# Two half-width GpSimd subtractions in place of one for the low parts of projection weights and keys

## What is computed

```
proj = x @ w_in                      # 5120 columns: q, k, v of two attentions, two gates
qa, ka, va -> stick_breaking(8 heads of 64)
    z = q k^T / 8;  a = exp(log_sigmoid(z) + suffix sum of log_sigmoid(-z));  y = a v
qb, kb, vb -> rope -> differential(4 heads, two maps each)
    w = softmax(z1) - lam * softmax(z2);  y = w v;  rms_norm
merged = sigmoid(ga) * (ya @ w_branch_a) + sigmoid(gb) * (yb @ w_branch_b)
x = layer_norm(ALPHA * x + merged @ w_out)
x = layer_norm(ALPHA * x + relu(x @ w_ff1)**2 @ w_ff2)
```

## Time and profile before

| | |
|---|---|
| time, median of 3 runs | 1521.79 us (1521.19 to 1521.81) |
| the profiled execution's own time | 1519.07 us |
| its span, first to last instruction | 1516.9 us |
| PE busy | 1475.1 us, 97% |
| DVE busy | 1007.9 us, 66% |
| ACT busy | 666.8 us, 44% |
| POOL busy | 328.2 us, 22%, 212 instructions |
| mean granted TensorE clock | 0.994 of full speed |

### The profile page before, as it was taken

How to read it: one execution, slowest core, us unless ns; L and a number is a source line. 1 busy time by engine, 2 the same in 40 slices (tenths; PEclk the granted TensorE clock), 3 DMA queues, 4 the chain that set the end, 5 groups by cost and what they waited for, 6 DMA issues and landing times. The chain is left out here.

```text
span 1516.9 us, 19312 instructions
## 1 busy us (share of the span) xinstructions
PE 1475.1 (97%) x7152; PEld 1226.8 (81%) x7152; DVE 1007.9 (66%) x1232; ACT 666.8 (44%) x1035; POOL 328.2 (22%) x212
## 2 busy tenths in 40 slices
PE   8999999999999998999999999999999999999997
PEld 7788888887887787888787877888888888888886
DVE  3677877779866556553346688766665467668767
ACT  3455554546556555443021344444444344433343
POOL 2535444446432223210130140000000000000004
PEclk9999999999999999998999999999999999999999
DMA  5101112111110000110452233644442677935553
GB/s 177 56 29 57 56 43 70 55 55 56 43 57 28 29 14 28 39 48 12 136 183 107 89 110 116 217 153 153 153 153 97 215 275 256 325 137 194 194 196 137
DMA packets 111503, 172.40 MB, mean 114 GB/s; under 512 B 6080, under 2 KB 71616, under 8 KB 111296
## 3 DMA queue, kind: packets, MB, share of 16 engines
q1 hardware_dynamic: 111424, 171.33, 33.2%
HBM read 127.27 MB, written 44.04 MB: 113 GB/s over the span
## 5 line engine op out<-in xcount | busy, mean ns | idle before, releaser
L756 PE MATMUL p_proj<-xt_h,w_hi 128*128 128x512 f32 x640 | 254.6, 398 | 0.2 <-DVE xt_l L1589 0.2
L760 PE MATMUL p_proj<-xt_h,w_lo 128*128 128x512 f32 x640 | 253.5, 396 | 0.0
L758 PE MATMUL p_proj<-xt_l,w_hi 128*128 128x512 f32 x640 | 252.1, 394 | 0.0
L2265 POOL TENSOR_TENSOR w_lo<-w_raw,w_hi 128x1024 fp32r<-128x1024 f32 x48 | 120.4, 2508 | 240.2 <-DVE w_hi L1596 239.7
L760 PEld LDWEIGHTS p_proj<-xt_h,w_lo 128*128 128x128 f32 x640 | 120.8, 189 | 23.6
L756 PEld LDWEIGHTS p_proj<-xt_h,w_hi 128*128 128x128 f32 x640 | 120.8, 189 | 22.4 <-DVE xt_l L1589 0.6
L758 PEld LDWEIGHTS p_proj<-xt_l,w_hi 128*128 128x128 f32 x640 | 120.9, 189 | 20.7
L2378 POOL TENSOR_TENSOR row_odd<-row_odd,gains 128x1024 f32<-128x1024 f32 x4 | 10.4, 2622 | 580.7 <-ACT row_odd L1561 580.7
L1589 DVE TENSOR_TENSOR d_al<-f_a,d_ah 128x1024 fp32r<-128x1024 f32 x56 | 68.5, 1224 | 79.5 <-ACT d_ah L1479 79.5
L1479 ACT ACTIVATE d_ah<-f_a 128x1024 fp32r<-128x1024 f32 x56 | 59.2, 1057 | 134.0 <-PE p_av L1130 54.9
L1328 ACT ACTIVATE a_t<-p_tr 128x384 fp32r<-128x384 f32 (+3 forms) x96 | 47.2, 491 | 123.4 <-PE p_tr L858 123.3
(11 more groups left out here) (287 smaller groups left out, 3537.1 us busy)
## 6 DMA issues: line engine op xcount, KB each, us to landing
f_a<-h_terms SPq DMA_DIRECT2D x56, 512.0 KB, 3.4
w_raw<-w_in SPq DMA_DIRECT2D x40, 512.0 KB, 3.9
h_terms<-c SPq DMA_DIRECT2D x40, 512.0 KB, 3.2
f_b<-w_ff SPq DMA_DIRECT2D x40, 512.0 KB, 4.9
r<-w_ff SPq DMA_DIRECT2D x32, 512.0 KB, 4.0
gate_rows<-gst SPq DMA_DIRECT2D x12, 512.0 KB, 5.0
y<-x SPq DMA_DIRECT2D x8, 512.0 KB, 7.8
wo_raw<-w_out SPq DMA_DIRECT2D x8, 512.0 KB, 8.8
```

Of the source, the lines that this page charges most:

```text
L756: pe.matmul(o, w_hi[n_slot][:, k, :], xt_h[:, k, cols], start=(k == 0), stop=False)
L758: pe.matmul(o, w_hi[n_slot][:, k, :], xt_l[:, k, cols], start=False, stop=False)
L760: mm = pe.matmul(o, w_lo[n_slot][:, k, :], xt_h[:, k, cols], start=False, stop=(k == KT - 1))
L2265: pool.tensor_tensor(w_lo[slot][:, :, :], w_raw[:, :, :], w_hi[slot][:, :, :].bitcast(F32), ALU.subtract).then_inc(wt_lo, 1)
```

## The change

POOL makes each low tile in two instructions. The 128 x 1024 subtraction of `tile_low` becomes two of 128 x 512 (the inner dimension's first four and last four blocks of 128), and the 64 x 1024 subtraction of `low_keys` two of 64 x 512 (columns 0 to 511 and 512 to 1023). The second one of each pair raises the semaphore that the single instruction raised. Nothing else differs, and the lines below it move down by two to four.

```diff
             def tile_low(n, slot):
 
                 pool.wait_ge(wt_hi, n + 1)
-                pool.tensor_tensor(w_lo[slot][:, :, :], w_raw[:, :, :], w_hi[slot][:, :, :].bitcast(F32),
-                                   ALU.subtract).then_inc(wt_lo, 1)
+                for ks in (slice(0, 4), slice(4, 8)):
+                    low = pool.tensor_tensor(w_lo[slot][:, ks, :], w_raw[:, ks, :], w_hi[slot][:, ks, :].bitcast(F32),
+                                             ALU.subtract)
+                low.then_inc(wt_lo, 1)
...
                     pool.wait_ge(st_dve, g * 4 + (m + 1))
-                    pool.tensor_tensor(k_lo[m][r, :], stage[1][r, :], k_hi[m][r, :].bitcast(F32), ALU.subtract)\
-                        .then_inc(st_pool, 1)
+                    for cols in (slice(0, NH), slice(NH, S)):
+                        low = pool.tensor_tensor(k_lo[m][r, cols], stage[1][r, cols], k_hi[m][r, cols].bitcast(F32),
+                                                 ALU.subtract)
+                    low.then_inc(st_pool, 1)
```

## The result

| | before | after |
|---|---|---|
| median of 6 runs | 1521.14 us (1518.93 to 1521.81) | 1511.40 us (1509.52 to 1513.23) |
| profiled execution | 1519.07 us | 1509.52 us |
| its span | 1516.9 us | 1507.4 us |
| mean granted clock of timed runs | 0.9932 (15 runs beside experiments 1 to 3) | 0.9965 |

What follows compares the result with a forecast made beforehand. PE, 97% busy, was taken to wait on DVE, itself held until POOL's whole instruction ended. Terms -3.3 - 0.3 - 1.3 + 0.9 - 1.7 = -5.7 us gave 1516.1 us; range 1512 to 1523.6, likeliest case 1511.8 to 1517.6.

Steps and rivals of the forecast that it cites:

- DVE gets in at the seam: Between POOL's two halves, the waiting DVE instruction goes after the first half; the forecast case, 56%.
- two rivals: DVE not let in between halves, 1523.4 us (19%); or extra instruction costs 0.36, nothing let in, 1525.8 us (7%).
- `be`, -3.3 and -0.3: PE's waits for `be`: 1.09 us sooner in each of groups 4 to 6, -3.3; group 7's wait gone, -0.3.
- `q_st`, -1.3: Group 0: DVE's cast and `q_st` alternate with POOL's halves, so PE's wait of 1.32 us goes.
- the case that the prediction named: Group 0: if POOL, not DVE's cast, goes first between the first two halves, `q_st` gains about 0.8 us.
- `a_t`, +0.9: Stick-breaking groups: DVE meets the second half, ending 0.15 us later; 0.15 charged to each of six waits.
- gains nothing: Stick-breaking groups: DVE and POOL meet at nearly every instruction, so alternating in finer pieces brings no gain.
- What a half costs, 0.15: Each POOL pair takes 0.15 us more than one whole instruction; first half 1.28 us.
- POOL busy near 345 us: Sign in the profile: POOL's busy time near 345 us, with 9.6 us from 64 splits.
- The keys' slack, 1.5 us left: Next differential group's keys end 2.7 us later than before, leaving 1.5 us before PE takes them.
- The clock, -1.7: Group 5: the fall to 1.2 GHz for 3.5 us behind the `be` wait disappears, saving 1.7 us.
- up to 3.4 us more: If timed runs held as many as three clock falls at the `be` waits, they would gain this extra.

Runs made afterwards that it cites:

- experiments 1 to 3: Changed kernel with only weight tiles halved, 1510.52 us; only key instructions halved, 1519.23; only four of 48 weight tiles halved, 1513.73; kernel before 1520.98.
- experiment 4: Only four weight tiles cut, at column 256 or at column 768 instead of 512: 1513.44 and 1514.52 us against 1521.13 for the kernel before.
- four tiles: Only the weight tile that `be` meets in each of groups 4 to 7 halved, all else whole: 1513.73 us against 1520.98 for the kernel before.
- the weights alone: Changed kernel with the keys in one instruction again, the 48 weight tiles still halved: 1510.52 us against 1520.98 for the kernel before.
- quarters: All 64 low-tile instructions in four pieces of 256 columns: 1509.58 us against 1520.98 for the kernel before, ratio 0.9927.
- Experiment 6: Kernel before plus eight discarded matmuls ahead of each of the three 2 us `be` waits: 1519.11 us against 1521.13, ratio 0.9991.
- experiment 5: Kernel before, whole POOL instructions, with DVE's cast of one weight tile per differential group issued after `be`'s L1713: 1516.02 us against 1521.13.
- both quarters: All 64 instructions in four pieces, without and with DVE's cast issued behind `be` in differential groups: 1509.58 and 1508.73 us; before, 1520.98 and 1520.66.
- Experiment 7: Sixteen discarded matmuls near 680 us, added to the kernel before with filled `be` waits and to the changed kernel: 1522.43 and 1518.86 us against 1520.66.
- experiment 2: Changed kernel with weight tiles whole again, only the 16 key instructions halved: 1519.23 us against 1520.98 for the kernel before, ratio 0.9994.

## Why the prediction was right on the waits and too small on the clock

- **DVE gets in at the seam** (56% forecast, against two rivals): right. Shown by the halves' 1.90 and 2.12 us and by the four places of the seam in experiment 4.
- **`be`, -3.3 and -0.3:** measured 6.4 to 2.9, -3.5. Group 7's wait of the earlier trace rows is gone, as said.
- **`q_st`, -1.3:** measured -0.8. It is the case that the prediction named: POOL won the first seam. Its four halves of `k_lo` ran from 40.69 to 46.75 and the cast, started at 43.97 inside a half, took 1.63 us; the wait before PE at 50.31 is 0.52.
- **`a_t`, +0.9:** the list of waits says +0.3, and in all it was a gain. The step charged a late seam to each of six waits, and four waits did rise by 0.14 or 0.15; two in group 3 fell, from 0.63 and 0.49 us to 0.36 and 0.24, by a trade of places that is shown below. From the `a_t` wait of group 2 to that of group 3 in the table above PE needs 97.38 us before and with four tiles, 96.75 with the weights alone, 96.53 with the change and 95.76 with quarters. So finer pieces do gain something in group 3, against the prediction's "gains nothing".
- **What a half costs, 0.15:** right. Two halves that meet nobody take 2.54 us against 2.39.
- **POOL busy near 345 us:** 351.7. The 9.6 us for the seams were in it; what POOL waits behind DVE was only named, and it is the rest of the rise of 23.5.
- **The keys' slack, 1.5 us left:** 1.9 left, nobody waits.
- **The waits together:** forecast -3.3 - 0.3 - 1.3 + 0.9 = -4.0. Measured -3.5 - 0.8 + 0.3 = -4.0 in the list, -5.3 in the table of matmuls, -3.6 and -4.4 at equal clock. Right in size, with some luck: `q_st` gained less and `a_t` cost less than forecast.
- **The clock, -1.7: this is the term that failed.** The mean granted clock of the timed runs rose from 0.9932 to 0.9965; 0.0033 of 1518 us is 5.0 us. This conversion is an estimate: it holds if PE works all through the falls, as the windows above show, and the 59 runs of the kernel before bear it out only roughly (4 at 0.992 average 1522.5 us, 40 at 0.993 1520.6, 12 at 0.994 1520.1, but 2 at 0.995 1521.9). The step priced the one fall of the earlier trace rows, which was gone as said. It left out the fall from 680.2 us in the same trace, which is three times as long, 10.2 us, and was 6.8 in the changed kernel's: 1.7 us that no term had. Further falls behind the `be` waits were named as a possibility, up to 3.4 us more, set in the low end and left out of the sum. Experiment 6 puts all falls behind these waits at 1.3 to 2.0 us a run, so the price of 1.7 for them was nearly right, by luck, since one execution holds one of them and another two. The other 3 us or so are at places of which the prediction said nothing.

The trade of places in group 3, in order of time; the kernel before:

```profile
347.83 0.64 POOL L2293 TENSOR_TENSOR y<-y,small 128x128 f32<-128x128 f32 x1
348.08 0.68 DVE L1680 TENSOR_TENSOR_SCAN y<-y,small 128x128 f32<-128x128 f32 x1
```

and the changed kernel:

```profile
343.62 1.51 DVE L1696 TENSOR_TENSOR y<-y 128x255 f32<-128x255 f32 x1
...
345.05 1.51 DVE L1680 TENSOR_TENSOR_SCAN y<-y,small 128x128 f32<-128x128 f32 x1
346.25 0.57 POOL L2297 TENSOR_TENSOR y<-y,small 128x128 f32<-128x128 f32 x1
...
348.03 0.41 PE L858 MATMUL p_tr<-small,y 128*128 128x128 f32 x2 [0.36 <-DVE a_t L1589]
```

Before, DVE's L1680 found POOL's `mask` (L2293) running. Now L1696, let in at the seam, is done sooner, L1680 waits behind the second half, and `mask` goes after it: DVE meets one POOL instruction less on the way to `a_t`.

The gain in the timed runs is then about 4 for the waits (3.6 and 4.4 by the two ways above), 1.3 to 2.0 for the falls behind them, about 3 for the clock elsewhere, and up to 1 of the 9.7 that none of these runs assigns.

**What stays open** is why the clock is granted more in the changed kernel where no `be` wait is near. In the profiles the fall in group 7 is 6.8 us long in place of 10.2, but one execution of each doesn't tell a cause. It isn't the keys (0.9933 with keys alone). The weights raise it: 0.9952, 0.9958 and 0.9957 in the three kernels with four tiles cut, 0.9964 and 0.9965 with all 48 in halves. But the later cast of experiment 5 raises it too, to 0.9956, and cuts nothing. The profiles, one of each kernel, don't sort by the cuts either: the fall of group 7 is 10.2 us long in the kernel before, with the keys alone, with four tiles and with quarters, and 6.8 in eight, the changed kernel and the later cast among them. Seven of the fourteen traces have one more fall, of 3.4 us, between 789 and 808 us: those of the weights alone, of both seams of experiment 4, of both quarters and of both kernels of experiment 7, but neither the kernel before nor the changed one. Two causes could be behind the higher clock, and they weren't told apart: that shorter waits shift the stages, so that the stretch of group 7 falls otherwise upon whatever the clock is decided by; or that many small PE gaps became shorter. Experiment 7 was made to remove that fall and failed. The quarters speak against a simple rule: their mean clock over the timed runs is 0.9944, lower than the halves', and their profile has a fall of 10.2 us from 669.1 and one of 3.4 from 792.0. They are no slower for it, since PE idles less: 36.7 us in all (1508.2 - 1471.5) against 38.3.

## What to carry to other kernels

Where two engines take turns at a shared port, the length of an instruction on the engine with time to spare is the latency of the other: find the instruction whose duration is too long for its size, see what it ended behind, and cut that one, not all of them; here four cuts brought 7.3 us where all 64 brought 9.7. Each cut has a price and moves the order behind it, so try two or three sizes: four pieces did as well as two here and eight lost nearly all the gain, when POOL itself came onto PE's path. And when a wait on TensorE goes, list every fall of the clock in the trace, not only the one beside the wait, and price them from the mean granted clock of many timed runs: one profile holds what one execution happened to have.

## What was unexpected of the hardware

- A seam with no semaphore is enough for the other engine to get the port: DVE's work there made POOL's second half take 2.12 us in place of 1.3, and DVE was let in at every place of the seam that was tried.
- A PE wait of about 2 us may or may not be followed by a fall to 1.2 GHz. Behind the same three waits (1.93 to 2.11 us) the kernel before showed one fall of about 3.5 us and experiment 2 showed two. Behind waits of 1.4 to 1.6 us the trace of the late seam shows none.
- The price of a seam is the same for one, three and seven of them, 0.14 or 0.15 us each. What made the eighths dear beyond it was POOL's pieces standing behind DVE.
